# A two-layer trunk with a mixture of experts: last products ahead of three row norms ordered by row block

## The chip, the cores and the metric

The kernel runs on one core of a Trainium2 chip, and the metric is the time of one execution in microseconds (us), median over the runs. All weights come from HBM in each execution.

## The reference

256 rows of 1024 channels pass two layers. Only the parts around the three norms that the change touches are written out:

```python
x = x + mla_attention(rms_norm(x, attn_norm[0]), ...)      # ends in o @ w_o
h = rms_norm(x, ffn_norm[0])                                # n1
x = x + (silu(h @ w1) * (h @ w3)) @ w2                      # dense, 2816 wide
h = rms_norm(x, attn_norm[1]); hkv = rms_norm(x, kv_norm)   # n2, one root for both
q, k, v = h @ w_q, hkv @ w_k, hkv @ w_v                     # each 1024 x 1024
x = x + attention(q, k, v) @ w_o
h = rms_norm(x, ffn_norm[1])                                # n3
x = x + top2_of_8_experts(h)                                # each 3584 wide
# rms_norm(x, g) = x / sqrt(mean(x*x) + 1e-6) * g, over the row
```

## The kernel before

**Numbers.** Products are made of split floats. A value is its high half (what fits the fast format `fp32r`) plus a low half; `mm3` (L1370) makes each product of three: high by high, high by low, low by high. Weights come in units of 128 x 2048 (1 MB), numbered in order of use: `U_WO0` (9) begins the first output projection, `U_FFN` (13) the dense FFN, `U_L1` (46) the q, k and v projections, `U_MOE - 4` (58) the second output projection, `U_MOE` (62) the experts. SyncE loads unit n into one of six buffers `raw`, when `lo(n - 6)` is done. `hi(n)` on ScalarE (L596) writes the unit's high half into one of three slots (six from U_MOE on), when the products that used the slot are done (`unit_used`); `lo(n)` on VectorE (L919) writes the low half; `ready(n)` lets TensorE wait for `lo(n)`.

**Rows.** The 256 rows are two blocks t of 128. The residual stream is `xr`. A norm (`norm(m)` on GpSimd, n1 to n3 for m = 1 to 3) runs so: `add_residual` on VectorE adds four PSUM banks, in the order (columns 0 to 511, t=0), (same, t=1), (512 on, t=0), (512 on, t=1); ScalarE squares each block's whole row with a sum into `ss` (L605); GpSimd makes the root of it in two steps (L488, L489); VectorE multiplies the block into `tn` (`normalise`, L925); TensorE transposes 2 x 8 squares into four PSUM banks (`turn`, L1365), the banks being handed on when both blocks are in; `turn_out` takes them out with the gain, high halves on ScalarE (L616) into `hth`, low halves on VectorE (L938) into `htl`. The queues of all engines are in order and written out by hand; there is no scheduler.

**Products before the norms.** `out_proj` runs over its four units (two column halves n, two depth halves h), both blocks in each; bank 4 + 2n + t holds the sums. The dense FFN runs eleven steps: `up(c)` uses two units, `down(c)` one; at step c TensorE does `up(c + 1)` and then `down(c)`, so that `f_gate`, `f_hi` and `f_lo` of c + 1 lie beside `down(c)`. The low half `f_lo` (L1136) stands behind a `lo` on VectorE. After n2, TensorE does the q projection (units U_L1 to U_L1 + 3), then k and v from `h2h`, `h2l`: a second set of halves with the gain of `kv_norm`, taken out of the same banks (L784, L1157), ahead of `hi` and `lo` of unit U_L1 + 2. After n3 come 16 router products (L1645), the choice of experts in small VectorE steps, the gathering of an expert's rows by products (L1667, `gathered`, L834 and L1204), and the runs of the experts. In a run, `combine` (L1693) puts the preceding expert's rows back in four parts over two banks; parts three and four wait for VectorE's adds of `add_run` (L1304), which stand behind the four `lo`s of units U_MOE + 4 to + 7.

Of the kernel before, what the change touches and what calls it, by code (L numbers as in the profile page):

```python
# [20 lines left out]
P = 128  # L21
D = 1024
SEQ = 256
T = SEQ // P
# [76 lines left out]
def trunk_kernel(nc, x, attn_norm, ffn_norm, w_dq, g_cq, w_uq, w_dkv, g_ckv, w_ukv, g_qn, g_kn, w_oa,  # L101
# [25 lines left out]
    with ctx:  # L127
# [212 lines left out]
        TURN = {"n0": 0, "a0": 1, "n1": 2, "n2": 3, "a1": 4, "n3": 5}  # L340
# [132 lines left out]
        def _(pool):  # L473
# [105 lines left out]
        def _(act):  # L579
# [27 lines left out]
            def turn_out(name, dsts):  # L607

                k = TURN[name]
                for b in range(TURN_BANKS):  # L610
                    act.wait_ge(tr_done, TURN_BANKS * k + b + 1)
                    for cc in range(2):
                        c = 2 * b + cc
                        for dst, g in dsts:
                            kw = {} if g is None else {"scale": gcol[:, g + c:g + c + 1]}
                            last = nc.scalar.activation(dst[:, c, :], ps[b][:, cc * SEQ:(cc + 1) * SEQ], ACT.Copy, **kw)  # L616
                    last.then_inc(th_done, 1)

            sum_squares(0, True)
# [4 lines left out]
            turn_out("n0", [(hth, G_ATT)])  # L624
# [142 lines left out]
            with act.Fori(0, (FSTEPS - 1) // 2) as j:  # L767
                for u in range(2):
# [5 lines left out]
                    f_hi(j * 2 + (u + 1), 1 - u)  # L774
            hi(U_L1 + 1)

            sum_squares(2, False)
            turn_out("n2", [(hth, G_ATT + DC)])

            for c in range(DC):  # L780
                if c % 2 == 0:

                    act.wait_ge(tl_done, TURN_BANKS * TURN["n2"] + c // 2 + 1)
# [28 lines left out]
            turn_out("a1", [(hth, None)])  # L812
# [90 lines left out]
        def _(dve):  # L903
# [18 lines left out]
            def normalise(m):  # L922
                for t in range(T):
                    dve.wait_ge(rstd_done, T * m + t + 1)
                    nc.vector.tensor_scalar(tn[:, t, :], xr[:, t, :], rstd[:, t:t + 1], None, ALU.mult).then_inc(tn_done, 1)  # L925

            def turn_out(name, dsts):
                k = TURN[name]
                for b in range(TURN_BANKS):
                    dve.wait_ge(th_done, TURN_BANKS * k + b + 1)  # L930
                    for cc in range(2):
                        c = 2 * b + cc
                        src = ps[b][:, cc * SEQ:(cc + 1) * SEQ]
                        for h, l, g in dsts:
                            if g is None:
                                last = nc.vector.tensor_tensor(l[:, c, :], src, h[:, c, :].bitcast(fp32), ALU.subtract)
                            else:
# [885 lines left out]
```

## Time and profile before

| | |
|---|---|
| median of 3 runs | 1520.61 us (1520.49 to 1523.8) |
| the profiled execution's own time | 1523.13 us |
| its span, first to last instruction | 1521.3 us |
| mean granted clock of TensorE | 0.977 |
| TensorE busy | 1451.0 us (95%) |
| VectorE busy | 1148.2 us (75%) |
| ScalarE busy | 954.7 us (63%) |
| GpSimd busy | 42.7 us (3%) |
| DMA | 424.67 MB, 279 GB/s mean; weight units land 5.1 to 7.3 us after issue |

"PE" is TensorE, "PEld" its weight loads, "DVE" VectorE, "ACT" ScalarE, "POOL" GpSimd, "SP" SyncE. A clock of 1.00 is 2.4 GHz, 0.50 is 1.2 GHz. Times on a timeline count from the start of the span. The first third of the span holds everything up to the first expert (to about 512 us); the rest is eight expert runs of some 125 us each.

### The profile page before, as it was taken

What the parts mean: (1) busy time and instruction counts of PE and PEld (TensorE: products, weight loads), DVE (VectorE), ACT (ScalarE), POOL (GpSimd) and SP (SyncE); (2) the same over time, 40 slices, a digit from 0 to 9 for tenths busy, and PEclk for the clock granted to TensorE, in tenths of its full rate; (3) what the DMA queues carried; (4) which work ended last, traced back from release to release, by engine and by line L of the source; (5) the groups of instructions that cost most, each with busy time, mean ns of one, the idle gap of its engine ahead of it and who ended that gap; (6) DMA issues with size and microseconds to landing.
All of it is one profiled execution on the core that took longest, in us unless ns stands there. A gap on an engine that the chain in (4) does not pass through costs nothing.

```text
span 1521.3 us, 20025 instructions
## 1 busy us (share of the span) xinstructions
PE 1451.0 (95%) x7249; PEld 1217.4 (80%) x7249; DVE 1148.2 (75%) x1049; ACT 954.7 (63%) x918; POOL 42.7 (3%) x79
## 2 busy tenths in 40 slices
PE   5788999998987899999999999999999999999998
PEld 5577999997876688878878878888887887887886
DVE  4665544546674889879888888888987998888894
ACT  4455433444563677767777777687776767677772
POOL 3120000000100000000000000000000000000000
PEclk9889999998999899999999999999999999999999
DMA  8145455554532599989989999998998998999992
GB/s 303 57 122 167 138 181 181 192 188 140 185 123 86 195 337 376 372 305 375 383 320 353 375 332 331 390 360 306 379 378 326 342 382 328 339 384 332 336 376 89
DMA packets 150625, 424.67 MB, mean 279 GB/s; under 512 B 11149, under 2 KB 41018, under 8 KB 150586
## 3 DMA queue, kind: packets, MB, share of 16 engines
q1 hardware_dynamic: 146752, 420.39, 76.0%
q10 hardware_dynamic: 3450, 3.69, 0.8%
q0 software_dynamic: 384, 0.07, 0.1%
q8 instruction: 24, 0.39, 0.1%
q14 instruction: 15, 0.12, 0.0%
HBM read 423.08 MB, written 4.19 MB: 281 GB/s over the span
## 4 chain that ended last, share of the span: by engine, by line
PE 93%; DVE 4%; ACT 1%; issue 1%; POOL 0%; DMA 0%; ACTq 0%; POOLq 0%; SPq 0%; DVEq 0%
PE ps L1370 82%; PE ps L1365 4%; PE ps L1693 2%; PE ps L1667 2%; PE ps L1484 2%; PE ps L1504 1%; DVE wl_a L919 1%; ACT wh_a L596 0%; DMA xr<-in_x 0%; ACT tn L605 0%; DVE kT L1047 0%; DVE bias L1062 0%; DVE xr L955 0%; PE ps L1645 0%; DVE htl L938 0%
## 5 line engine op out<-in xcount | busy, mean ns | idle before, releaser
L919 DVE TENSOR_TENSOR wl_a<-raw,wh_a 128x2048 fp32r<-128x2048 f32 (+1 forms) x230 | 516.0, 2270 | 123.1 <-ACT wh_a L596 123.1
L596 ACT ACTIVATE wh_a<-raw 128x2048 fp32r<-128x2048 f32 (+1 forms) x230 | 434.1, 1906 | 209.6 <-PE ps L1370 200.3
L919 DVE TENSOR_TENSOR wl_b<-raw,wh_b 128x2048 fp32r<-128x2048 f32 x168 | 378.8, 2286 | 35.4 <-ACT wh_b L596 34.3
L596 ACT ACTIVATE wh_b<-raw 128x2048 fp32r<-128x2048 f32 x168 | 319.3, 1925 | 56.5 <-PE ps L1370 53.3
L1370 PE MATMUL ps<-wh_a,hth 128*128 128x512 f32 (+2 forms) x576 | 226.3, 393 | 5.6 <-DVE htl L938 3.5
L1370 PE MATMUL ps<-wl_a,hth 128*128 128x512 f32 (+2 forms) x576 | 223.4, 388 | 0.0
L1370 PE MATMUL ps<-wh_a,htl 128*128 128x512 f32 (+2 forms) x576 | 223.4, 388 | 0.0
L1370 PE MATMUL ps<-wh_b,hth 128*128 128x512 f32 x448 | 178.4, 398 | 0.0
L1370 PE MATMUL ps<-wh_b,htl 128*128 128x512 f32 x448 | 174.6, 390 | 0.0
L1370 PE MATMUL ps<-wl_b,hth 128*128 128x512 f32 x448 | 174.4, 389 | 0.0
L1370 PEld LDWEIGHTS ps<-wh_a,hth 128*128 128x128 f32 x576 | 109.3, 190 | 30.1 <-issue 6.7
L1370 PEld LDWEIGHTS ps<-wh_a,htl 128*128 128x128 f32 x576 | 109.2, 190 | 21.6
L1370 PEld LDWEIGHTS ps<-wl_a,hth 128*128 128x128 f32 x576 | 109.4, 190 | 20.5
L854 ACT ACTIVATE gth<-ps 128x512 fp32r<-128x512 f32 x56 | 30.8, 595 | 139.5 <-PE ps L1365 139.5
L1370 PE MATMUL ps<-hth,wh_a 128*128 128x256 f32 x352 | 100.5, 286 | 1.1 <-DVE htl L938 1.1
L1370 PE MATMUL ps<-htl,wh_a 128*128 128x256 f32 x352 | 100.4, 285 | 0.0
L1370 PE MATMUL ps<-hth,wl_a 128*128 128x256 f32 x352 | 100.3, 285 | 0.0
L1370 PEld LDWEIGHTS ps<-wl_b,hth 128*128 128x128 f32 x448 | 84.2, 188 | 18.9 <-issue 1.9
L1370 PEld LDWEIGHTS ps<-wh_b,hth 128*128 128x128 f32 x448 | 84.1, 188 | 18.9 <-issue 1.9
L1370 PEld LDWEIGHTS ps<-wh_b,htl 128*128 128x128 f32 x448 | 84.1, 188 | 17.6
L1370 PE MATMUL ps<-wh_b,gth 128*128 128x512 f32 x224 | 88.0, 393 | 1.3 <-DVE gtl L1285 1.3
L1370 PE MATMUL ps<-wh_b,gtl 128*128 128x512 f32 x224 | 87.3, 390 | 0.0
(230 smaller groups left out, 2050.9 us busy)
## 6 DMA issues: line engine op xcount, KB each, us to landing
raw<-in_moe_w SPq DMA_DIRECT2D x336, 1024.0 KB, 7.3
raw<-in_ffn_w SPq DMA_DIRECT2D x33, 1024.0 KB, 5.3
raw<-in_a_w_o SPq DMA_DIRECT2D x4, 1024.0 KB, 5.7
raw<-in_b_w_q SPq DMA_DIRECT2D x4, 1024.0 KB, 5.1
raw<-in_kv_w_k SPq DMA_DIRECT2D x4, 1024.0 KB, 5.1
raw<-in_kv_w_v SPq DMA_DIRECT2D x4, 1024.0 KB, 5.0
raw<-in_b_w_o SPq DMA_DIRECT2D x4, 1024.0 KB, 5.2
bias<-bias_wide ACTq DMA_DIRECT2D x8, 384.0 KB, 3.2
```

Source lines behind the costliest of these rows:

```text
L596: nc.scalar.activation(dst[:, 0:w], raw[:, n % RAW, 0:w], ACT.Copy).then_inc(hi_done, 1)
L854: last = nc.scalar.activation(gth[:, b * 512:(b + 1) * 512], ps[6 + b][:, :], ACT.Copy)
L919: nc.vector.tensor_tensor(l[:, 0:w], raw[:, n % RAW, 0:w], h[:, 0:w].bitcast(fp32), ALU.subtract).then_inc(lo_done, 1)
L1365: return nc.tensor.transpose(dst, src, ident[0:np_, 0:np_])
L1370: last = mm(dst, b if flip else a, a if flip else b, start=start and i == 0, stop=stop and i == 2)
L1484: last = mm(ps[2 + h][:, lo_:lo_ + keys], qT[part, par, q_at + t * P:q_at + (t + 1) * P], kT[part, par, h * SEQ:h * SEQ + keys], start=Tru ...
L1504: last = mm(dst, probT[:, par, h, (t + kt) * P:(t + kt + 1) * P], v_src[:, kt:kt + 1, ds(p * 2 + h, 1), v_at:v_at + VDIM], start=kt == 0, ...
L1667: last = mm(ps[7 - g][:, cc * P:(cc + 1) * P], tn[:, t, c * P:(c + 1) * P], pick[:, t, :], start=t == 0, stop=t == T - 1)
L1693: mm(ps[6 + i % 2][:, :], cmb[:, t * P:(t + 1) * P], ye[:, n * 512:(n + 1) * 512], start=True, stop=True).then_inc(m_cmb, 1)
```

## The change

- `turn_part` turns one block; a `turn_out` can be for one block; `TURN` counts n1 to n3 as two turns each. The banks are those of before.
- Squares are taken by half rows, each after its add; GpSimd scales the first half's sum ahead and adds the second's.
- In `out_proj`, unit 0 serves both blocks, units 1 to 3 block 0, then 1 to 3 block 1; block 0's transposes stand ahead of the last of these.
- In the FFN, `up` of the last step comes ahead of both last `down`s, and these run by block; block 0's transposes stand ahead of the last quarter of them.
- The first two projection units are used by block 0 first, then come block 1's transposes, then block 1.
- Adds, norms, turn outs and some `hi` and `lo` change places; `lo(U_MOE + 1)` to `+ 3` each move back by one place in VectorE's queue.

```diff
--- before.py
+++ after.py
...
-        TURN = {"n0": 0, "a0": 1, "n1": 2, "n2": 3, "a1": 4, "n3": 5}
+        TURN = {"n0": 0, "a0": 1, "n1": 2, "n2": 4, "a1": 6, "n3": 7}
...
+            for t in range(T):
+                pool.wait_ge(ss_done, t + 1)
+                root(rstd[:, t:t + 1], ss[:, t:t + 1], D).then_inc(rstd_done, 1)
+
             def norm(m):
+
                 for t in range(T):
-                    pool.wait_ge(ss_done, T * m + t + 1)
-                    root(rstd[:, t:t + 1], ss[:, t:t + 1], D).then_inc(rstd_done, 1)
-
-            norm(0)
+                    done = T + 4 * (m - 1) + 2 * t
+                    part, whole = rstd[:, T + t:T + t + 1], rstd[:, t:t + 1]
+                    pool.wait_ge(ss_done, done + 1)
+                    chain(nc.gpsimd.tensor_scalar(part, ss[:, t:t + 1], 1.0 / D, EPS, ALU.mult, ALU.add))
+                    pool.wait_ge(ss_done, done + 2)
+                    chain(nc.gpsimd.tensor_scalar(whole, ss[:, T + t:T + t + 1], 1.0 / D, part, ALU.mult, ALU.add))
+                    nc.gpsimd.tensor_tensor(whole, whole, negh[:, 0:1], ALU.pow).then_inc(rstd_done, 1)
...
-            def sum_squares(m, first):
-                for t in range(T):
-                    if first:
-                        act.wait_ge(x_here, 16 * T)
-                    else:
-
-                        act.wait_ge(xr_done, 4 * (m - 1) + 3 + t)
-                    nc.scalar.activation(tn[:, t, :], xr[:, t, :], ACT.Square, accum_out=ss[:, t:t + 1]).then_inc(ss_done, 1)
-
+            def half_squares(m, t, n):
+
+                act.wait_ge(xr_done, 4 * (m - 1) + 2 * t + n + 1)
+                piece = slice(n * 512, (n + 1) * 512)
+                nc.scalar.activation(tn[:, t, piece], xr[:, t, piece], ACT.Square,
+                                     accum_out=ss[:, n * T + t:n * T + t + 1]).then_inc(ss_done, 1)
+
+            def turn_out(name, dst, g, t=None):
...
-            turn_out("a0", [(hth, None)])
-            for n in range(U_WO0 + 2, U_FFN + 2):
-                hi(n)
-
-            sum_squares(1, False)
+            turn_out("a0", hth, None)
+            hi(U_WO0 + 2)
+            hi(U_WO0 + 3)
+            half_squares(1, 0, 0)
+            half_squares(1, 0, 1)
+            hi(U_FFN)
+            half_squares(1, 1, 0)
+            turn_out("n1", hth, G_FFN, 0)
+            hi(U_FFN + 1)
+            half_squares(1, 1, 1)
             hi(U_FFN + 2)
-            turn_out("n1", [(hth, G_FFN)])
+            turn_out("n1", hth, G_FFN, 1)
...
+            half_squares(2, 0, 0)
+            half_squares(2, 0, 1)
             hi(U_L1 + 1)
-
-            sum_squares(2, False)
-            turn_out("n2", [(hth, G_ATT + DC)])
+            turn_out("n2", hth, G_ATT + DC, 0)
+            half_squares(2, 1, 0)
+            half_squares(2, 1, 1)
+            turn_out("n2", hth, G_ATT + DC, 1)
...
+            half_squares(3, 0, 0)
+            half_squares(3, 0, 1)
+            half_squares(3, 1, 0)
+
+            act.wait_ge(unit_used, U_MOE - 1)
+            hi(U_MOE, w=UNIT)
+            turn_out("n3", hth, G_FFN + DC, 0)
+            half_squares(3, 1, 1)
+            turn_out("n3", hth, G_FFN + DC, 1)
             act.wait_ge(unit_used, U_MOE)
-            hi(U_MOE, w=UNIT)
-            sum_squares(3, False)
-            hi(U_MOE + 1, w=UNIT)
-            turn_out("n3", [(hth, G_FFN + DC)])
-            for k in range(2, 4):
+            for k in range(1, 4):
                 hi(U_MOE + k, w=UNIT)
...
+            def add_piece(t, n, done, value):
+
+                dve.wait_ge(done, value)
+                piece = xr[:, t, n * 512:(n + 1) * 512]
+                nc.vector.tensor_tensor(piece, ps[4 + 2 * n + t][:, :], piece, ALU.add).then_inc(xr_done, 1)
...
-            for n in range(U_WO0 + 1, U_FFN + 2):
+            turn_out("a0", hth, htl, None)
+            for n in range(U_WO0 + 1, U_FFN):
                 lo(n)
-            add_residual(0, U_WO0 + 4, U_WO0 + 2)
-            normalise(1)
+            add_piece(0, 0, y_done[0], 1)
+            add_piece(0, 1, y_done[0], 2)
+            normalise(1, 0)
+            add_piece(1, 0, unit_used, U_WO0 + 2)
+            lo(U_FFN)
+            turn_out("n1", hth, htl, G_FFN, 0)
+            add_piece(1, 1, unit_used, U_WO0 + 4)
+            lo(U_FFN + 1)
+            normalise(1, 1)
+            turn_out("n1", hth, htl, G_FFN, 1)
             lo(U_FFN + 2)
-            turn_out("n1", [(hth, htl, G_FFN)])
...
+            add_piece(0, 0, y_done[1], 1)
+            add_piece(0, 1, y_done[1], 2)
+            normalise(2, 0)
+            add_piece(1, 0, y_done[1], 3)
+            turn_out("n2", hth, htl, G_ATT + DC, 0)
+            add_piece(1, 1, unit_used, U_L1)
             lo(U_L1 + 1)
-            add_residual(1, U_L1)
-
-            normalise(2)
-            turn_out("n2", [(hth, htl, G_ATT + DC)])
+            normalise(2, 1)
+            turn_out("n2", hth, htl, G_ATT + DC, 1)
...
-            add_residual(2, U_MOE, U_MOE - 2)
+            add_piece(0, 0, y_done[2], 1)
+            add_piece(0, 1, y_done[2], 2)
+            normalise(3, 0)
+            add_piece(1, 0, unit_used, U_MOE - 2)
+            turn_out("n3", hth, htl, G_FFN + DC, 0)
+            add_piece(1, 1, unit_used, U_MOE)
             lo(U_MOE, w=UNIT)
-            normalise(3)
-            lo(U_MOE + 1, w=UNIT)
-            turn_out("n3", [(hth, htl, G_FFN + DC)])
+            normalise(3, 1)
+            turn_out("n3", hth, htl, G_FFN + DC, 1)
...
-            lo(U_MOE + 2, w=UNIT)
+            lo(U_MOE + 1, w=UNIT)
...
-            lo(U_MOE + 3, w=UNIT)
             gathered(0)
+            lo(U_MOE + 2, w=UNIT)
...
+            lo(U_MOE + 3, w=UNIT)
...
+            def turn_part(name, t, sem_, value, part):
+
+                pe.wait_ge(sem_, value)
+                for b in range(TURN_BANKS):
+                    for cc in range(2):
+                        c = 2 * b + cc
+                        last = tr(ps[b][:, cc * SEQ + t * P:cc * SEQ + (t + 1) * P], tn[:, t, c * P:(c + 1) * P])
+                    if part:
+                        last.then_inc(tr_done, 1)
...
+                ready(u0)
+                for t in range(T):
+                    last = piece(0, t)
+                last.then_inc(unit_used, 1)
+
+                for i in range(1, 4):
+                    ready(u0 + i)
+                    last = piece(i, 0)
+                    if i != 2:
+                        last.then_inc(y_done[2 * la], 1)
+                for i in range(1, 4):
+                    if i == 3:
+                        turn_part(then, 0, tn_done, 4 * la + 3, True)
+                    piece(i, 1).then_inc(unit_used, 1)
...
+            turn_part("n1", 1, tn_done, 4, True)
...
-            with pe.Fori(1, (FSTEPS - 1) // 2) as j:
+            with pe.Fori(1, (FSTEPS - 1) // 2 - 1) as j:
                 for u in range(2):
                     ffn_step(j * 2 + u, u, U_FFN + 2 + 3 * u, j=j, j_units=6)
-            down(FSTEPS - 1, 0, U_L1 - 1, False, True)
-
-
-            turn("n2", [(tn_done, 5), (tn_done, 6)])
-            i = 0
+            ffn_step(FSTEPS - 3, 0, U_FFN + 2 + 3 * (FSTEPS - 3))
+            up(FSTEPS - 1, 0, U_FFN + 2 + 3 * (FSTEPS - 2))
+
+
+            for t in range(T):
+                for c, par, n in ((FSTEPS - 2, 1, U_L1 - 2), (FSTEPS - 1, 0, U_L1 - 1)):
+                    if t == 0:
+                        ready(n)
+                        pe.wait_ge(f_gl, c + 1)
+                    wh, wl = split_slot(n)
+                    for half in range(2):
+                        for f in range(2):
+                            g = slice(f * SEQ + t * P, f * SEQ + (t + 1) * P)
+                            at = f * D + half * 512
+                            last = mm3(ps[4 + 2 * half + t][:, :], fgh[:, par, g], fgl[:, par, g],
+                                       wh[:, at:at + 512], wl[:, at:at + 512], False, c == FSTEPS - 1 and f == 1)
+                        if c == FSTEPS - 1 and (half, t) != (1, T - 1):
+                            last.then_inc(y_done[1], 1)
+                        if c == FSTEPS - 1 and t == T - 1 and half == 0:
+
+                            turn_part("n2", 0, tn_done, 5, True)
+                    if t == T - 1:
+                        last.then_inc(unit_used, 1)
+            def project(w, n, h, t):
...
+            for h in range(2):
+                ready(U_L1 + h)
+                project(0, 0, h, 0)
+            turn_part("n2", 1, tn_done, 6, True)
+            for h in range(2):
+                project(0, 0, h, 1).then_inc(unit_used, 1)
...
+            out_proj(1, U_MOE - 4, "n3")
+
+
+            turn_part("n3", 1, tn_done, 8, True)
...
```

## Rows read from the trace of the kernel before

**Rows 1.** Page, chain that ended last, shares of the span by engine

```profile
PE 93%; DVE 4%; ACT 1%; issue 1%; POOL 0%; DMA 0%; ACTq 0%; POOLq 0%; SPq 0%; DVEq 0%
```

**Rows 2.** The chain in order of time: start us, us, what

```profile
352.96 62.52 PE ps L1370 x264
...
611.68 16.34 PE ps L1370 x72
```

**Rows 3.** Timeline of TensorE at n1: start, us, instruction, count, [idle before, released by]

```profile
151.79 1.09 PE L1365 MATMUL ps<-cst,tn 128*128 128x128 f32 x8 [3.72 <-DVE tn L925]
153.27 1.97 PE L1365 MATMUL ps<-cst,tn 128*128 128x128 f32 x8 [0.38 <-DVE tn L925]
156.35 0.55 PE L1370 MATMUL ps<-hth,wh_a 128*128 128x256 f32 x1 [1.11 <-DVE htl L938]
```

**Rows 4.** Timeline of TensorE at n2

```profile
348.64 3.68 PE L1365 MATMUL ps<-cst,tn 128*128 128x128 f32 x16 [3.63 <-DVE tn L925]
352.96 0.77 PE L1370 MATMUL ps<-wh_a,hth 128*128 128x512 f32 x1 [0.65 <-DVE htl L938]
```

**Rows 5.** Timeline of TensorE at n3

```profile
488.96 3.68 PE L1365 MATMUL ps<-cst,tn 128*128 128x128 f32 x16 [5.80 <-DVE tn L925]
493.51 0.37 PE L1645 MATMUL ps<-hth,wrs 128*16 128x256 f32 x1 [0.87 <-DVE htl L938]
```

**Rows 6.** Stretches: length, busy by engine, granted clock, DMA share, GB/s

```profile
346.00:348.00 2.00, 0.00 (x0) 0.00 (x0) 0.47 (x2) 1.92 (x4) 0.74 (x2) 0.96 1.04 407
358.00:360.00 2.00, 2.00 (x9) 1.63 (x9) 1.46 (x2) 0.81 (x1) 0.00 (x0) 0.98 0.03 8
```

**Rows 7.** Timeline of ScalarE, n2 and after: a square, a copy

```profile
345.74 1.06 ACT L605 ACTIVATE tn<-xr 128x1024 f32<-128x1024 f32 x1 [4.15 <-DVE xr L955]
...
366.55 0.60 ACT L797 ACTIVATE q_all<-ps 128x512 f32<-128x512 f32 x1 [3.46 <-PE ps L1370]
```

**Rows 8.** Timeline of GpSimd, n2 and n3

```profile
346.97 0.19 POOL L488 TENSOR_SCALAR rstd<-ss 128x1 f32<-128x1 f32 x1 [194.54 <-ACT tn L605]
347.25 0.55 POOL L489 TENSOR_TENSOR rstd<-rstd,negh 128x1 f32<-128x1 f32 x1
...
486.24 1.25 POOL L488 TENSOR_SCALAR rstd<-ss 128x1 f32<-128x1 f32 x1 [44.13 <-ACT tn L605]
```

**Rows 9.** Timeline of VectorE, n2 and n3: adds, normalise, a `lo`

```profile
343.82 2.48 DVE L955 TENSOR_TENSOR xr<-ps,xr 128x512 f32<-128x512 f32 x4
347.83 0.75 DVE L925 TENSOR_SCALAR tn<-xr,rstd 128x1024 f32<-128x1024 f32 x1 [1.53 <-POOL rstd L489]
...
485.15 2.29 DVE L919 TENSOR_TENSOR wl_a<-raw,wh_a 128x2048 fp32r<-128x2048 f32 x1 [1.25 <-ACT wh_a L596]
```

**Rows 10.** Timelines of VectorE and ScalarE, last FFN steps: `lo(U_L1)`, `f_lo(10)`, `hi(U_L1+1)`

```profile
336.09 2.30 DVE L919 TENSOR_TENSOR wl_a<-raw,wh_a 128x2048 fp32r<-128x2048 f32 x1 [1.17 <-ACT wh_a L596]
338.30 0.69 DVE L1136 TENSOR_TENSOR fgl<-fg,fgh 128x512 fp32r<-128x512 f32 x1
...
339.67 1.92 ACT L596 ACTIVATE wh_a<-raw 128x2048 fp32r<-128x2048 f32 x1 [3.09 <-PE ps L1370]
```

**Rows 11.** Timeline of ScalarE after n2: the second set of high halves

```profile
353.94 3.07 ACT L784 ACTIVATE h2h<-ps,gcol 128x256 fp32r<-128x256 f32 x8
```

**Rows 12.** Timeline of ScalarE, first expert: high halves of gathered rows

```profile
508.06 1.14 ACT L834 ACTIVATE hth<-ps,gcol 128x128 fp32r<-128x128 f32 x4 [6.87 <-PE ps L1667]
```

**Rows 13.** Timeline of VectorE, first expert: `lo(U_MOE+3)`, gathered rows, two `lo`s, `add_run`

```profile
506.81 2.29 DVE L919 TENSOR_TENSOR wl_b<-raw,wh_b 128x2048 fp32r<-128x2048 f32 x1
...
511.20 1.13 DVE L1204 SCALAR_TENSOR_TENSOR htl<-ps,gcol,hth 128x128 fp32r<-128x128 f32 x4 [0.84 <-ACT hth L834]
...
515.64 4.64 DVE L919 TENSOR_TENSOR wl_b<-raw,wh_b 128x2048 fp32r<-128x2048 f32 x2 [1.78 <-ACT wh_b L596]
...
524.61 1.50 DVE L1304 TENSOR_TENSOR xr<-ps,xr 128x512 f32<-128x512 f32 x2
```

**Rows 14.** Timeline of TensorE, first expert: `combine`

```profile
523.50 3.83 PE L1693 MATMUL ps<-ye,cmb 128*128 128x512 f32 x8
```

More of the change, by code:

```diff
@@ L920, in lo, with normalise @@
                                         ALU.subtract).then_inc(lo_done, 1)
[L922 to L928, printed above, removed]
+            def normalise(m, t):
+                dve.wait_ge(rstd_done, T * m + t + 1)
+                nc.vector.tensor_scalar(tn[:, t, :], xr[:, t, :], rstd[:, t:t + 1], None, ALU.mult).then_inc(tn_done, 1)
@@ L940, in turn_out @@
-                    last.then_inc(tl_done, 1)
-            def add_residual(block, used, first_half=None):
-                for n in range(2):
-                    for t in range(T):
-                        i = 2 * n + t
-                        if i == 3:
-                            dve.wait_ge(unit_used, used)
-                        elif n == 0 and first_half is not None:
-                            dve.wait_ge(unit_used, first_half)
-                        else:
-                            dve.wait_ge(y_done[block], i + 1 if first_half is None else 1)
-                        piece = xr[:, t, n * 512:(n + 1) * 512]
-                        nc.vector.tensor_tensor(piece, ps[4 + i][:, :], piece, ALU.add).then_inc(xr_done, 1)
@@ L957, in _ @@
-            normalise(0)
+                        part = slice(lo_, lo_ + n_)
+                        src = ps[b][:, cc * SEQ + lo_:cc * SEQ + lo_ + n_]
+                        if g is None:
+                            last = nc.vector.tensor_tensor(l[:, c, part], src, h[:, c, part].bitcast(fp32), ALU.subtract)
+                        else:
+                            last = nc.vector.scalar_tensor_tensor(l[:, c, part], src, gcol[:, g + c:g + c + 1],
+                                                                  h[:, c, part].bitcast(fp32), ALU.mult, ALU.subtract)
@@ L1371, in mm3, with turned @@
                 return last
[L1373 to L1384 removed]
+            def turn_part(name, t, sem_, value, part):
[6 more added lines that the diff above has]
+                        last.then_inc(tr_done, 1)
+            def turned(name, c=DC - 1, first=True, t=0):
                 if first:
[L1387 removed]
+                    pe.wait_ge(tl_done, TURN_BANKS * (TURN[name] + t) + c // 2 + 1)
             def ready(n, j=0, j_units=0):
@@ L1394, in _ @@
             pe.wait_ge(c_here, 16)
-            turn("n0", [(tn_done, 1), (tn_done, 2)])
+            for t in range(T):
+                turn_part("n0", t, tn_done, t + 1, t == T - 1)
             pe.wait_ge(g_here, 16 * 5)
@@ L1558, in _ @@
             for _ in attention(0):
                 pass
-            turn("a0", 2 * [(A[0]["oo"], PAIRS)])
-            out_proj(0, U_WO0)
-            turn("n1", [(tn_done, 3), (tn_done, 4)])
+            for t in range(T):
+                turn_part("a0", t, A[0]["oo"], PAIRS, t == T - 1)
+            out_proj(0, U_WO0, "n1")
+            turn_part("n1", 1, tn_done, 4, True)
             def up(c, par, n, j=0, j_units=0, first=False):
@@ L1590, in down @@
                                        wh[:, at:at + 512], wl[:, at:at + 512], first and f == 0, last_ and f == 1)
-                        if last_ and (half, t) != (1, T - 1):
-                            last.then_inc(y_done[1], 1)
                 last.then_inc(unit_used, 1)
@@ new lines, in _ @@
+            for t in range(T):
+                for c, par, n in ((FSTEPS - 2, 1, U_L1 - 2), (FSTEPS - 1, 0, U_L1 - 1)):
[15 more added lines that the diff above has]
+                        last.then_inc(unit_used, 1)
@@ new lines, in project @@
+            def project(w, n, h, t):
+                xh, xl = (hth, htl) if w == 0 else (h2h, h2l)
+                i = 4 * w + 2 * n + t
+                wh, wl = split_slot(U_L1 + 4 * w + 2 * n + h)
+                if h == 0:
+                    free_bank(i, 1)
+                for cc in range(4):
+                    c = 4 * h + cc
+                    turned("n2", c, w == 0 and n == 0 and c % 2 == 0, t)
+                    if w == 1 and n == 0 and t == 0 and c % 2 == 0:
+                        pe.wait_ge(h2_done, c // 2 + 1)
+                    last = mm3(ps[4 + i % 4][:, :], xh[:, c, t * P:(t + 1) * P], xl[:, c, t * P:(t + 1) * P],
+                               wh[:, cc * 512:(cc + 1) * 512], wl[:, cc * 512:(cc + 1) * 512], c == 0, c == DC - 1)
+                return last
```

96 lines of the change are left out of this document (33 added, 63 removed).

## The prediction

> **What bounds the kernel now.** I read the page's chain of work by engine first [rows 1]: TensorE holds 93% of it, so only stretches in which TensorE waits, or runs at the lower clock, can give time back. The chain in order of time gives the price of a product at full clock: 72 of 512 columns in 16.34 us, 0.227 us each [rows 2]. Twelve of them, half a weight unit for one row block, I call a piece: 2.72 us. Then the timeline of TensorE at the three seams where a row norm follows the last products; the idle time in front of the transposes tells when those products ended:
> - FFN norm (n1): end at 151.79 - 3.72 = 148.07, first `up` product at 156.35 [rows 3]: 8.28 us.
> - second layer's attention norm (n2): end 345.01, first projection product 352.96 [rows 4]: 7.95 us.
> - MoE norm (n3): end 483.16, first router product 493.51 [rows 5]: 10.35 us.
>
> Together 26.6 us, of which only the 16 transposes of each are work. The stretches at n2 show the clock too: it falls from 2.4 towards 1.2 GHz while TensorE is idle (mean 0.96 over 346 to 348) and is back at 358 (0.98) [rows 6]. The projections from 352.96 took 62.52 us for 264 products without a break, where 264 x 0.227 = 59.9 [rows 2]: 2.6 us of slow clock. The 16 transposes took 3.68 us there [rows 4], against 1.09 for eight at full speed [rows 3], 1.5 more.
>
> **Prices.** A square over 1024 columns holds ScalarE 1.06 us; a half lies between half of that, 0.53, and the 0.60 of a 128x512 copy [rows 7]; I take 0.6, and 0.1 for the sum. GpSimd's two steps are 0.19 and 0.55 [rows 8]. Normalise is 0.75 per block; four adds are 2.48 [rows 9], one alone I put at 0.7. The high halves of a 128x128 turn out took 1.14 for four [rows 12]; a block has eight, 2.3 us on ScalarE, and VectorE follows one pair behind. A `hi` is 1.92 [rows 10], a `lo` 2.29 [rows 9], 2.25 in a series.
>
> GpSimd's 0.19 us step took 1.25 us at 486.24, to 487.49 [rows 8], and the `lo` that VectorE had begun at 485.15 ended at 487.44 [rows 9]: beside a `lo` this step waits for its end. The change puts a `lo` between the last add and the last scaling of all three seams, and I count that wait; were the row an accident, the sum would be 2.1 us lower (a rival below). The Trainium skill has it as a rule, in SBUF — State Buffer, Who interferes with whom: a VectorE instruction with two SBUF inputs keeps out a GpSimd one that reads SBUF. By that rule, the trace agrees.
>
> **n1.** The new order keeps the eight pieces and makes block 0's last one the fifth, which ends at 148.07 - 3 x 2.72 = 139.9. Its add, half square, root and normalise end near 143.1, ahead of the seventh piece's end at 145.35; so the block's eight transposes (1.0 to 1.1 us) stand between products, and the last product ends at E = 149.1. After E: add to E+0.75, `lo(U_FFN+1)` to E+2.95 (its `hi` runs on ScalarE from 147.9 to 149.8), and though the square is there at E+1.5, GpSimd is kept out till E+2.95; root to E+3.55, normalise to E+4.3. Then block 1's transposes, a first bank of 0.5 at the slow clock, ScalarE's pair 0.6, VectorE's pair 0.6, with hand-overs 1.95 to 2.0: first `up` product at E+6.3 = 155.4. Gain 0.95. The other order bound: no transposes hidden and no shorter chain, nothing.
>
> **n2.** `up(10)` ends at 345.01 - 10.9 (two `down`s of 5.44) = 334.1. Then come both last `down`s for block 0, and both for block 1. The second for block 0 needs `f_lo(10)`, which stands behind `lo(U_L1)` on VectorE and ends at 338.99 [rows 10]; before, the whole of `down(9)`, 5.4 us, was its cover, now half of it, to 336.8: a new stall of 2.3 us. From 339.1, block 0's two column halves end at 340.4 and 341.8 and its norm is ready at 345.2; `down` of block 1 runs on to 345.8, the transposes to 346.8, the last half of it to 348.2, 3.2 later than before. ScalarE turns block 0 out from 346.5 (behind `hi(U_L1+1)`), so the first projection piece runs 348.2 to 350.9. The second needs `lo(U_L1+1)`, now behind block 0's turn out and the last add on VectorE: 350.0 to 352.25. TensorE waits 1.45 and runs to 355.1. Block 1 is normalised at 353.6, kept out as above; its transposes end at 356.1, TensorE waits 0.7 for its turn out, and its two pieces run 356.8 to 362.2. What is late next: `h2h`, `hi` and `lo` of unit U_L1+2, which stand behind block 1's turn out. ScalarE: turn out 355.5 to 357.8, `h2h` 3.0 [rows 11], `hi` 1.9, to 362.7; `lo` to 365.0. That unit's products start at 365.1, where they started at 352.96 + 2 x 5.44 + 2.6 = 366.5. Gain 1.4, of the 4.3 us by which the pieces before it were early.
>
> **n3.** As n1, but `hi(U_MOE)` (1.9) runs ahead of block 0's turn out on ScalarE, which ends at 484.7, VectorE's at 485.3. Last product 484.2, one set of transposes later; add 485.3 to 486.0, `lo(U_MOE)` to 488.2, GpSimd kept out till then, root 488.8, normalise 489.55, first router product 489.6 + 1.95 = 491.5. Gain 2.0.
>
> **First expert.** Here I expect n3's gain to be given back. The `lo`s of units U_MOE+1 to +3 each move back by one place. Before, `lo(U_MOE+3)` ran at 506.81 [rows 13], while VectorE had to wait for ScalarE's part of the gathered rows (508.06 [rows 12]) anyway; nothing takes its place. Now two `lo`s, 4.5 us, stand between `gathered(0)` and the run, where VectorE was idle for 1.78 [rows 13]. On the old clock: gathered rows done 512.3, `lo` 514.6, gates 1.55, `lo` 518.4, four `lo`s of 2.25 to 527.4. Behind them is `add_run`, which began at 524.61 [rows 13]. In TensorE's `combine`, eight products in 3.83 us from 523.50 [rows 14], the third pair waits for the first add and the fourth for the second. So it ends near 528.2 + 1.95 = 530.1 instead of 527.33: 2.8 us lost. The register loads ahead of the run's loop lay in the 1.78 us of idleness and no longer do: 0 to 1.8 us, 0.3 taken, as an engine's hand-overs in these rows are nearer to nothing. Loads of units U_MOE+8 on start up to 9 us later, but lie several units ahead of their use; nothing, and if that cover were gone a load's landing (5 to 7 us on the page). The two more squares of each norm and GpSimd's extra 0.19 us step lie in pauses of their engines and cost nothing; on the path each would be 0.6 and 0.2.
>
> **Sum.** -0.95 - 1.4 - 2.0 + 2.8 + 0.3 = -1.3 us. The profiled execution took 1523.13 us, its span 1521.3; the sum against its own time is 1521.8. The median of the runs is 1520.61, 2.5 below it; where that lies I can't show (the runs spread over 3.3 us, about what a slow clock at one seam costs). Forecast by the median: 1519.3.
>
> **Rivals.**
> - *The first expert's backlog doesn't reach TensorE*: 3.1 less, 1516.2. For: VectorE had 1.78 us of idleness there. Against: from 506.8 on I count 17.3 us of work for it where 15.1 stood. 18%.
> - *GpSimd isn't kept out by a `lo`*: n1 ends 0.75 earlier, n3 1.35, n2 the same: 1517.2. Against: the 1.25 us row [rows 8]. 7%.
> - *Slower: the clock falls in the new stall of n2.* The price is that of n2's slow stretch now, 2.6 us [rows 2], or 4.1 with the transposes; 3.4 taken: 1522.7. It decides whether the clock falls at all at a stall of 2.3 us between dense products. For: it fell after a pause of 3.72 us with only transposes behind it (the second eight took 1.97 [rows 3]). Against: that pause was longer. 15%. The Trainium skill (TensorE: Matmul & The Clock Gate, Why this matters for your kernels) warns of pauses longer than this one; by it the clock would hold, and no row here shows a pause of this length.
> - *The change doesn't do what it says*: block 0 is early, but block 1's chain is as long as the old one and no seam gains: 1520.6 + 3.1 = 1523.7. Against: that chain has half a square and half a turn in it. 10%.
>
> The forecast has 50%. A measurement of this kernel can tell about 0.3%, 4.6 us, from no change: the bounds are 1516.05 and 1525.2. Faster: half of the first rival and some of the second and of the forecast's low end, 0.13. Slower: the high ends of the last two (4.1, and register loads of 1.8), 0.06. Within it, 0.81. The range of 1515.8 to 1523.8 reaches to the first rival and to the last.
>
> **What would show it.** Right: TensorE idle for 2.3 us ahead of block 0's second `down`, behind `fgl`; 1.5 us behind `wl_a` between the two first projection pieces, and near 3 us ahead of unit U_L1+2; GpSimd's last scaling in n1 and n3 ending with a `lo`; the first expert's `combine` waiting near 3 us for `xr`. Wrong: a `combine` without that wait, a granted clock below 1 from 339 on, or block 0's transposes waiting for their normalise.

## The result: slower than forecast, and slower than before

| | before | after |
|---|---|---|
| timed together with the first profile | 1521.83 us | 1526.95 us (1526.3 to 1527.64, 6 runs) |
| ratio | | 1.0034, 95% interval [1.0022, 1.0045] |
| timed again, beside the kernel before | 1522.18 us | 1525.64 us (1524.51 to 1526.94, 11 runs), 1.0021 [1.0012, 1.003] |
| profiled execution, span | 1523.13, 1521.3 | 1526.84, 1525.0 |
| mean granted clock | 0.977 | 0.982 |

The forecast was 1519.3, with a range to 1523.8: wrong in sign, and the time lies outside. The slowdown is small, 0.2 to 0.3%, but both intervals lie above 1. Yet nearly every wait that the forecast listed is in the trace. At n1, TensorE's timeline of the changed kernel (start, us, instruction, [idle before, released by]) and below it GpSimd's last scaling and VectorE's `lo`:

```profile
146.51 1.03 PE L1394 MATMUL ps<-cst,tn 128*128 128x128 f32 x8
154.85 1.97 PE L1394 MATMUL ps<-cst,tn 128*128 128x128 f32 x8 [4.57 <-DVE tn L945]
156.99 0.55 PE L1399 MATMUL ps<-hth,wh_a 128*128 128x256 f32 x1 [0.17 <-DVE htl L959]
...
151.94 1.43 POOL L503 TENSOR_SCALAR rstd<-ss,rstd 128x1 f32<-128x1 f32 x1 [3.60 <-ACT tn L610]
...
150.94 2.29 DVE L939 TENSOR_TENSOR wl_a<-raw,wh_a 128x2048 fp32r<-128x2048 f32 x1
```

They answer to [rows 3]: block 0's transposes stand between products with no wait. From the last product (154.85 - 4.57 = 150.28) to the first `up` product are 6.71 us, where 6.3 were forecast and 8.28 stood before. GpSimd's step ends at 153.37, 0.14 behind the `lo`. At n3, which answers to [rows 5], it is 7.60 us for 10.35:

```profile
491.42 1.97 PE L1394 MATMUL ps<-cst,tn 128*128 128x128 f32 x8 [5.46 <-DVE tn L945]
493.56 0.37 PE L1717 MATMUL ps<-hth,wrs 128*16 128x256 f32 x1 [0.17 <-DVE htl L959]
```

At n2, which answers to [rows 4], TensorE waits four times, for 6.4 us together:

```profile
339.13 0.47 PE L1399 MATMUL ps<-wh_a,fgh 128*128 128x512 f32 x1 [2.28 <-DVE fgl L1156]
354.02 0.50 PE L1399 MATMUL ps<-wh_a,hth 128*128 128x512 f32 x1 [1.23 <-DVE wl_a L939]
358.64 0.50 PE L1399 MATMUL ps<-wh_a,hth 128*128 128x512 f32 x1 [0.71 <-DVE htl L959]
366.60 0.50 PE L1399 MATMUL ps<-wh_a,hth 128*128 128x512 f32 x1 [2.22 <-DVE wl_a L939]
```

In the first expert, `add_run` begins only as the fourth `lo` of the run ends, at 526.7, and `combine` waits for it; these rows of VectorE and TensorE answer to [rows 13, 14]:

```profile
522.30 4.48 DVE L939 TENSOR_TENSOR wl_a<-raw,wh_a 128x2048 fp32r<-128x2048 f32 x2
526.71 1.28 DVE L1333 TENSOR_TENSOR xr<-ps,xr 128x512 f32<-128x512 f32 x2
...
527.44 3.30 PE L1765 MATMUL ps<-ye,cmb 128*128 128x512 f32 x4 [2.47 <-DVE xr L1333]
```

What the forecast doesn't have is in the granted clock. The stretches of the changed kernel (length, busy by engine, then granted clock, DMA share, GB/s) behind the first, the fourth and the combine's wait:

```profile
340.00:341.00 1.00, 1.00 (x5) 0.77 (x4) 0.00 (x0) 0.00 (x0) 0.00 (x0) 0.62 0.76 256
341.00:343.00 2.00, 2.00 (x6) 1.52 (x5) 0.69 (x1) 0.72 (x2) 0.19 (x1) 0.50 0.96 375
344.00:346.00 2.00, 2.00 (x10) 1.67 (x9) 0.37 (x1) 0.72 (x2) 0.62 (x2) 1.00 0.00 0
...
366.00:367.00 1.00, 0.40 (x2) 0.36 (x3) 1.00 (x2) 1.00 (x3) 0.00 (x0) 1.00 0.00 0
368.00:370.00 2.00, 2.00 (x6) 1.51 (x6) 2.00 (x3) 0.31 (x1) 0.00 (x0) 0.50 0.76 295
372.00:374.00 2.00, 2.00 (x10) 1.66 (x9) 0.00 (x0) 0.00 (x0) 0.00 (x0) 1.00 1.05 386
...
526.00:527.00 1.00, 0.00 (x0) 0.00 (x0) 1.00 (x2) 1.00 (x2) 0.00 (x0) 1.00 0.94 365
528.00:531.00 3.00, 3.00 (x6) 1.33 (x5) 0.91 (x2) 0.00 (x0) 0.00 (x0) 0.50 1.02 407
532.00:534.00 2.00, 2.00 (x11) 1.62 (x10) 2.00 (x2) 0.10 (x1) 0.00 (x0) 1.00 0.67 274
```

Three times TensorE goes on at full clock for 0.5 to 1.1 us after the wait, is granted 0.50 (1.2 GHz) while its work is dense, and comes back after some 3.4 us. Over 341 to 343 the row counts 6 products where it otherwise counts 10 or 11.

Do such falls come in dense work anyway? Two long stretches of the changed kernel, of the dense FFN and of the experts, answer that; in them TensorE is busy all the time:

```profile
162.50:335.00 172.50, 172.50 (x1242) 163.70 (x1241) 82.19 (x51) 68.85 (x52) 0.00 (x0) 1.00 0.56 184
535.00:1494.00 959.00, 959.00 (x4400) 787.39 (x4400) 827.49 (x573) 694.72 (x521) 0.00 (x0) 1.00 0.95 352
```

The granted clock is 1.00 in both, and so it is in the same stretches of all 18 profiles of this case.

**The span in sections.** To sum this, I cut each profile at six products of TensorE and its end: the first of the first output projection, the first `up` product (n1), the first of the second output projection (n2), the first of the router (n3), the first of the first expert, and the first behind its `combine`. Mean over four profiles of the kernel before and five of the changed order (one with its last loop steps written out, see below), in us; the spread of each in brackets (a page gives the span to 0.1 us, so the last section is good to 0.05):

| section | before | after | difference | forecast |
|---|---|---|---|---|
| to the output projection | 126.40 (126.07-126.87) | 126.78 (125.78-127.73) | +0.4 | 0 |
| n1 | 30.29 (30.28-30.31) | 29.63 (29.62-29.65) | -0.66 | -0.95 |
| dense FFN, n2, attention | 304.59 (302.93-305.82) | 306.06 (305.24-307.02) | +1.47 | -1.4 |
| n3 | 32.38 (32.37-32.39) | 30.53 (30.51-30.53) | -1.85 | -2.0 |
| router, gathering | 18.89 (18.68-19.01) | 18.62 (18.16-19.38) | -0.27 | 0 |
| first expert up to its `combine` | 14.29 (14.29-14.30) | 17.54 (16.80-17.91) | +3.25 | +3.1, with the next |
| the rest | 994.58 (994.54-994.64) | 995.14 (994.57-995.39) | +0.56 | |

The sum is +2.9, for +3.5 and +5.1 timed. The first section is code that the change doesn't touch, and its two spreads overlap.

### The profile page after: what moved, and what is told of

It is laid out like the page before. It is cut to its first block, busy times and chain, and to the rows that moved or that the text cites. A ratio compares the mean times of both kernels' runs of the same rounds, so it can differ in the third digit from the quotient of the medians.

```text
span 1525.0 us, 20089 instructions
## 1 busy us (share of the span) xinstructions
PE 1450.9 (95%) x7249; PEld 1214.9 (80%) x7249; DVE 1151.2 (75%) x1073; ACT 960.3 (63%) x954; POOL 47.7 (3%) x85
## 4 chain that ended last, share of the span: by engine, by line
PE 91%; DVE 5%; ACT 2%; issue 1%; DMA 1%; POOL 0%; DVEq 0%; ACTq 0%; POOLq 0%; SPq 0%
PE ps L1399 80%; PE ps L1394 4%; PE ps L1765 2%; PE ps L1739 2%; PE ps L1513 2%; DVE wl_a L939 1%; PE ps L1533 1%; ACT wh_a L604 1%; DVE htl L959 1%; DMA xr<-in_x 0%; ACT hth L621 0%; DVE kT L1060 0%; DVE bias L1075 0%; PE ps L1717 0%; DMA bias<-bias_wide 0%
```

## The experiments

All but five were timed in 5 to 11 runs of their own beside 16 to 27 of the kernel before, whose median was 1522.13 to 1522.34; a profiled execution of each gives the sections. "Below" is below the changed kernel's 1525.64. The other five are one profiled execution each.

**The kernel before, again** (one profiled execution).

> The kernel before, once more, for a second profile. In the first one the chain reached the first output projection at 126.07 us, in the changed kernel's profile at 127.34, with nothing of the change ahead of it. If that 1.3 us is chance (where the slow clock falls in the unchanged start), this profile will show another start, anywhere from 125.5 to 128.5, while the stretch from that first output product to the first up product stays at 30.3 us and the one from there to the router's first product at 337.2, each within the 2 us that a slow clock can take. If it belongs to the change, the start stays within 0.3 us of 126.07.

1524.74 us, span 1522.9. The start is 126.57 for 126.07, more than the 0.3 that would have tied it to the change, so it varies by itself. The section with n2 is 305.82 for 304.79; the granted clock fell at places where nothing had changed (424.5 and 458.5 us).

**`f_lo(10)` ahead of `lo(U_L1)`.** The last two FFN steps of ScalarE's and VectorE's loop are written out and two instructions change places in the last one (excerpt, against the written-out form):

```diff
-                lo(n + 2, FSTEPS // 2 - 1, 6)
                 f_lo(FSTEPS - 2 + u, 1 - u)
+                lo(n + 2, FSTEPS // 2 - 1, 6)
```

(for u = 1, where n + 2 is U_L1; `hi` and `f_hi` alike).

> The changed kernel, with the high and low halves of the last FFN step's gated product taken ahead of the hi and lo of unit U_L1 instead of behind them (the last two steps of two loops written out for it). Theory 1, the clock falls after the 2.3 us stall ahead of block 0's second down: stall and slow stretch both go, the granted clock stays 1.00 from 330 to 350, block 0's second down ends 3.9 us earlier (2.3 of stall, 1.6 of slow clock), and the kernel takes 1526.95 - 3.9 = 1523.0 us, unless the wait ahead of unit U_L1+2 grows by as much. Theory 2, the slow stretch there was chance and would come anyway: 2.3 us less, 1524.7. If neither the stall nor the clock was on the path (the chain of block 1's turn out sets it): 1526.95.

1519.7 us (1518.95 to 1521.1), ratio 0.9984 [0.9975, 0.9993]: 5.9 below, far more than the wait of 2.3 that is gone. TensorE's timeline has no wait behind `fgl`, and in this execution the clock held behind the other two as well, though they are still there. The wait at unit U_L1 + 2, and then the stretch behind it:

```profile
362.03 0.50 PE L1419 MATMUL ps<-wh_a,hth 128*128 128x512 f32 x1 [2.21 <-DVE wl_a L949]
```

```profile
363.00:365.00 2.00, 2.00 (x10) 1.64 (x10) 2.00 (x3) 0.73 (x1) 0.00 (x0) 1.00 0.71 257
```

The section with n2 is 302.16 us. My expectation counted the wait and one fall; in the profile two more falls are missing. From the first output projection product on, this profile is 4.3 below the mean of the changed order's five; 1.6 of the 5.9 isn't in it.

**`lo(U_MOE + 2)` back ahead of the gathered rows.**

```diff
-            gathered(0)
             lo(U_MOE + 2, w=UNIT)
+            gathered(0)
```

> The changed kernel, with lo(U_MOE+2) back in VectorE's idle time ahead of the gathered rows, where lo(U_MOE+3) stood before the change. Theory 1 (the backlog of two lo behind the gathered rows reaches combine): add_run begins 2.2 us earlier, the wait of 2.47 us inside the first combine falls to some 0.3, and since the clock no longer falls behind that wait another 1 to 1.5 us comes back: 1526.95 - 3.6 = 1523.3. Theory 2 (only the wait, the slow clock comes anyway): 1524.8. If combine is set by something else: 1526.9, and the wait stays.

1521.73 us, 0.9993 [0.9984, 1.0002]: 3.9 below. VectorE's `lo` fills the time in which it waited for ScalarE, and the combine's wait is 0.27 (timelines of VectorE and TensorE):

```profile
505.29 2.29 DVE L939 TENSOR_TENSOR wl_a<-raw,wh_a 128x2048 fp32r<-128x2048 f32 x1
507.51 1.13 DVE L1232 SCALAR_TENSOR_TENSOR htl<-ps,gcol,hth 128x128 fp32r<-128x128 f32 x4
...
523.75 1.98 PE L1765 MATMUL ps<-ye,cmb 128*128 128x512 f32 x4 [0.27 <-DVE xr L1333]
```

The last two sections together are 1009.23, and in before 1008.83 to 1008.93. So all but 0.4 us of the backlog is that one `lo`.

**n2 in the old order** (both last `down`s, all transposes, then the projection; squares by half rows and everything at n1 and n3 kept).

> The changed kernel with the second seam (end of the FFN, norm n2, first two projection units) ordered as before, n1 and n3 as changed. In the changed kernel's profile n2 is worth +1.4 us against before, by two stalls of 2.2 to 2.3 us and two slow stretches that cost 1.6 us each. Theory 1: so this one takes 1526.95 - 1.4 = 1525.5, a little more or less by the chance of one slow stretch in the old order. Rival (n2 gained its 1.4 us as predicted, and the loss is elsewhere): 1528.4.

1523.13 us, 1.0007 [0.9998, 1.0016]: 2.5 below, where my theory had 1.4 and its rival a loss. Its n2 section, 302.64, is under before's too. With the squares by half rows the chain is shorter: the wait ahead of the transposes is 2.78 for 3.63 [rows 4], and the first eight of these ran at full clock (timeline of TensorE):

```profile
346.21 1.10 PE L1392 MATMUL ps<-cst,tn 128*128 128x128 f32 x8 [2.78 <-DVE tn L944]
348.04 1.86 PE L1392 MATMUL ps<-cst,tn 128*128 128x128 f32 x8 [0.73 <-DVE tn L944]
350.56 0.77 PE L1397 MATMUL ps<-wh_a,hth 128*128 128x512 f32 x1 [0.65 <-DVE htl L958]
```

By the split into clock and remainder that is made below, the clock is what this section gained: 4.0 us lost to it for 6.6 in before, and a remainder of 298.6 for 297.8 to 298.3.

**The changed kernel again, and a control** with the same loop steps written out and the order left as it is.

> The changed kernel once more, beside the kernel before on the same chip. If the 5 us by which it came out slower belong to its code, the ratio is again 1.003 (some 1526.5 us for 1522). If a part of them belongs to the start of that one chip (its first output projection stood 1.3 us later than in the kernel before, in code that the change does not touch), the ratio is 1.001 to 1.002. In its profile the stall at the first gate product of the last unit is 2.3 us, the one at unit U_L1+2 2.2 and the combine's 2.5; where the granted clock falls to 0.5 behind one of them it stays there for 3.4 us.

> The changed kernel with the loops of its last steps written out and the order of every instruction left as it is: the control for the kernels whose steps were reordered. It computes and issues the same, so every theory expects the time of the changed kernel within 0.1%. If it is 2 us faster, then the 1519.7 of the kernel with f_lo first was partly the written-out form.

1525.64 us and 1526.21 us (1.0024 [1.0015, 1.0033]): writing the steps out gives nothing. The two have the same order, and yet the clock held behind `fgl` in the changed kernel's profile and fell in the control's (from each, the wait and the stretch behind it):

```profile
339.01 0.47 PE L1399 MATMUL ps<-wh_a,fgh 128*128 128x512 f32 x1 [2.28 <-DVE fgl L1156]
340.00:343.00 3.00, 3.00 (x15) 2.47 (x14) 1.38 (x2) 0.97 (x3) 0.19 (x1) 1.00 0.88 333
...
339.60 0.47 PE L1413 MATMUL ps<-wh_a,fgh 128*128 128x512 f32 x1 [2.35 <-DVE fgl L1163]
341.00:344.00 3.00, 3.00 (x9) 2.35 (x8) 0.69 (x1) 0.72 (x2) 0.19 (x1) 0.50 0.77 298
```

**GpSimd left free.** `lo(U_FFN + 1)` at n1 and `lo(U_MOE)` at n3 stand behind block 1's splits (excerpt, the one at n1):

```diff
-            lo(U_FFN + 1)
             normalise(1, 1)
             turn_out("n1", hth, htl, G_FFN, 1)
+            lo(U_FFN + 1)
```

> The changed kernel with lo(U_FFN+1) of the first norm and lo(U_MOE) of the third moved behind block 1's splits, so that VectorE runs no cast-and-subtract while GpSimd has its last scaling. If that scaling is 1.43 and 1.40 us long because VectorE's split keeps GpSimd out, it falls to 0.2 to 0.3 us, the last normalise starts about 1.2 us earlier, and block 1's turns in both norms too: 0.8 to 1.2 us at each, 1.6 to 2.4 less than the changed kernel in all, if nothing else is late. The rival (GpSimd's step is long of itself) leaves the time as it is.

1523.31 us, 1.0002 [0.9993, 1.0011]: 2.3 below. GpSimd's scaling falls from 1.43 to 0.27, and the wait ahead of block 1's transposes from 4.57 to 3.41 (timelines of GpSimd and TensorE):

```profile
152.22 0.27 POOL L503 TENSOR_SCALAR rstd<-ss,rstd 128x1 f32<-128x1 f32 x1 [3.60 <-ACT tn L610]
...
153.97 1.97 PE L1394 MATMUL ps<-cst,tn 128*128 128x128 f32 x8 [3.41 <-DVE tn L945]
```

n3 gains the same (29.40 us for 30.53). By the Trainium skill (SBUF — State Buffer, Who interferes with whom) a VectorE instruction with two SBUF inputs contends with a GpSimd one that reads SBUF. By that rule, the trace agrees: only the two `lo`s moved, and the scaling fell by 1.16 us.

**Unit U_L1 + 2 split ahead of block 1's turn out**, loops written out as in the control (excerpt).

```diff
+            lo(U_L1 + 2)
             turn_out("n2", hth, htl, G_ATT + DC, 1)
```

(`hi` alike, and both left out of the loop behind).

> The changed kernel with one thing moved: hi and lo(U_L1+2), the split of the third projection unit, stand ahead of block 1's turns instead of behind block 1's splits. In the changed kernel the unit's first product waits 2.2 us for it, and the clock fell to 0.5 for 3.4 us behind that wait in each of its profiles. If that is 2.2 + 1.7, the time is 3.5 to 4 below the changed kernel's, 1521.5 to 1522, and the section from the first up product to the second attention's output projection 302 instead of 305.2 to 306.0. The rival (the split moved ahead makes block 1's turns or splits late by as much): no change.

1522.63 us, 1.0003 [0.9994, 1.0012]: 3.0 below, and the n2 section is 301.28 for 305.24 in the changed kernel's second profile, in neither of which the clock fell at the first wait. The 4.0 are the wait of 2.2 and one fall, 1.7; why the runs gave 1 less than this pair of profiles stays open.

**Two orders together** (`f_lo` first, `lo(U_MOE + 2)` back).

> f_lo first and lo(U_MOE+2) back ahead of the gathered rows, nothing else. Alone they came out 5.9 and 3.9 us below the changed kernel (1519.7 and 1521.7 for 1525.6). If their stalls and the clock behind them add up: 1515.8 and, against the fastest, 3 us are left for unit U_L1+2 and GpSimd's steps. The rival (the gains overlap, since f_lo first also kept the clock up at the combine by moving it in time): 1517.3, the combine's 2.5 alone being added.

1517.33 us (1516.49 to 1518.07), 0.9969 [0.9957, 0.9981]: 8.3 below, where 9.8 would be the sum, and just what the rival expected: a part of what `f_lo` first gained was the clock at the combine. The one profile of `f_lo` first agrees; its other ten runs can't show it. Here the clock fell behind the 2.19 us at unit U_L1 + 2, as it had not with `f_lo` first alone (the wait and the stretch behind it):

```profile
360.92 0.50 PE L1419 MATMUL ps<-wh_a,hth 128*128 128x512 f32 x1 [2.19 <-DVE wl_a L949]
362.00:365.00 3.00, 3.00 (x9) 2.33 (x8) 3.00 (x3) 0.62 (x1) 0.00 (x0) 0.50 0.94 318
```

**All four.**

> All reorderings together: f_lo(10) first, lo(U_MOE+2) back ahead of the gathered rows, hi and lo(U_L1+2) ahead of block 1's turns, and the two splits that keep GpSimd out moved behind. My theory (the change gains 0.6 and 1.9 us at the first and third norm and loses it all to three stalls that it opens itself, of 2.2 to 2.5 us each, and to the clock that falls behind them): without the three stalls 1518.5 us, with the two splits moved another 1 to 2, 1517 to 1518, 0.3% faster than before. The rival (the loss is spread, or a stall comes back elsewhere): 1520 to 1522.

1512.82 us (1512.18 to 1514.13), 0.9934 [0.992, 0.9948]: faster than both kernels, by more than I expected (1517 to 1518). The four taken alone add up to 15.1 below; together they are 12.8. Its timeline at n2 has two waits left, and the clock stays up (the stretch behind the first):

```profile
349.09 0.50 PE L1423 MATMUL ps<-wh_a,hth 128*128 128x512 f32 x1 [1.14 <-DVE wl_a L951]
353.70 0.50 PE L1423 MATMUL ps<-wh_a,hth 128*128 128x512 f32 x1 [0.70 <-DVE htl L971]
```

```profile
350.00:352.00 2.00, 2.00 (x11) 1.58 (x10) 2.00 (x2) 0.00 (x0) 0.00 (x0) 1.00 0.95 225
```

Its sections: n1 28.26, n2 300.15, n3 29.38, expert 14.61, rest 994.58.

**The same without one of the four.**

> All reorderings at the first norm, the third and the experts as in the fastest kernel so far (1512.8), but the second norm in its old order (all last products, then all turns, then the projection; squares by half rows kept). That section was 302.6 us long in the kernel with this order alone and 300.15 in the fastest, so the block order of the second norm, with its stalls mended, is worth 2.5: 1515.3. The rival (without its stalls the block order is worth nothing, and the difference was the other edits): 1512.8 to 1513.5.

> The fastest kernel with lo(U_MOE+2) put back behind the gathered rows, so that the first combine waits for xr again. The wait itself is 2.5 us; in the changed kernel's four profiles the clock fell behind it, and it cost 4.1 to 4.3 from the first expert product on; in the two kernels where it did not fall, 2.5. So 1515.3 without a fall, 1517 with one, and the section from the first expert product to the first linear product 16.8 or 17.7 us for 14.6.

n2 in the old order: 1516.6 us (1514.69 to 1517.59), 3.8 slower than the fastest (2.5 expected), so the block order there is good once its long waits are gone. The profiles show less of it: 301.48 us for the section, beside 300.15 with all four and 298.24 in the kernel below, which has the same order at n2. `lo(U_MOE + 2)` behind the gathered rows: 1516.69 us (1514.88 to 1519.72), 3.9 slower; the combine waits 2.46 and the clock falls, sections 17.74 and 995.22 (the wait and the stretch behind it):

```profile
517.32 3.35 PE L1789 MATMUL ps<-ye,cmb 128*128 128x512 f32 x4 [2.46 <-DVE xr L1357]
518.00:521.00 3.00, 3.00 (x6) 1.36 (x5) 0.99 (x2) 0.00 (x0) 0.00 (x0) 0.50 1.03 416
```

**Two more profiles of each kernel**, for what the sections left open.

> The kernel before, one more profile. Both its profiles so far came from executions above its median (1523.13 and 1524.74 for 1522.2), with 10 us at half clock behind the second norm or with falls in dense work. If such executions are the exception, the section from the first up product to the second attention's output projection is 302.6 to 304 us here instead of 304.8 and 305.8, with 7 us at half clock, and the whole from the first up product on 1394 or less instead of 1395.2 and 1396.3. If they are the rule, 304.8 or more.

> As the one above: the kernel before, to see how the clock behind the second norm varies from one execution to the next.

> The changed kernel, one more profile. Its profiles gave 305.2 to 306.0 us from the first up product to the second attention's output projection, the clock falling at unit U_L1+2 in each, and at the first stall in two of three; and 1396.7 to 1397.8 from the first up product on. The theory expects the same here, and the fall at the combine again.

> As the one above: the changed kernel, to see whether a fall behind one of its three stalls is ever missing.

1521.89, 1523.18, 1526.16 and 1525.54 us. The n2 section took 302.93 and 304.82 in before, 305.95 and 307.02 in the changed kernel; so of before's four profiles three are the longer kind and one the shorter. From the first output projection product on, before takes 1393.2 to 1396.3 us in four profiles and the changed kernel 1396.7 to 1397.9 in five: they don't overlap. The sections account for 2.9 us; 0.6 of one timed difference and 2.2 of the other stay open. In the last profile the clock held at the combine, and that shows what a fall costs there. Stretches of it, to be put beside 528 to 531 above:

```profile
526.00:528.00 2.00, 0.29 (x1) 0.29 (x2) 2.00 (x3) 2.00 (x2) 0.00 (x0) 1.00 0.94 356
529.00:531.00 2.00, 2.00 (x9) 1.39 (x8) 1.83 (x3) 0.00 (x0) 0.00 (x0) 1.00 1.02 420
```

## Why the prediction was wrong, by its own steps

The forecast's base was low: a median of three runs, 1520.61, where more runs gave 1521.8 to 1522.3. So 1.2 us or more of the miss is none of the change's. What the change itself did was forecast at -1.3 and came out at +3.5 and +5.1.

**The waits were right.** Stall behind `fgl`: 2.3 forecast, 2.28. Wait for `lo(U_L1 + 1)`: 1.45, 1.23. Block 1's turn out: 0.7, 0.71. Unit U_L1 + 2: from 362.2 to 365.1, near 3; measured 2.22. `combine`: near 3, measured 2.47. GpSimd kept out: 1.43, 1.40, 1.40 us at the three norms, and shown at n1 and n3 by the kernel that frees it, so that rival falls. So does the one of a backlog that doesn't reach TensorE, and the one by which no seam gains. n1 gave 0.3 less: block 1's transposes began 4.57 behind the last product for 4.3, and from them to the first `up` product it took 2.14 for 1.95 to 2.0. n3 gave 0.15 less.

**The step that failed is the price of a wait between dense products.** The sum took each new wait at its own length. Three of them, of 2.2 to 2.5 us, stand with full work on both sides, and the clock fell behind most: over all profiles of all kernels that have the wait, behind `fgl` in 5 of 8, at unit U_L1 + 2 in 8 of 9, at the combine in 7 of 10. One of the forecast's own signs of being wrong, a granted clock below 1 from 339 on, came true. The size is plain at the combine, where little else varies. The last two sections are 1008.83 to 1008.93 in before, 1011.37 to 1011.41 in the three profiles with the wait and no fall, 1012.93 to 1013.10 in the seven with both. The wait is 2.5, the fall 1.6: 3.4 us at half clock. The forecast had 3.1 there: 0.6 too much for the wait, and nothing for the fall, 1.6.

**n2: the gain was a gain of clock.** Adding up (1 - granted clock) x length over stretches of half a microsecond gives what each section lost at the lower clock; in the n2 section it is 5.1 to 7.5 in before's profiles (mean 6.6) and 3.9 to 6.2 in the changed kernel's (4.7). The remainder is 297.8 to 298.3 before and 300.8 to 301.5 after. (`f_lo` first, alone and with the `lo` back, has one order at n2 and gave 298.2 and 298.9, so this split is good to some 0.7.) So waits cost 3.3 more, and the clock gave 1.9 back. The sum holds the end of the fall behind n1 too, which reaches over the cut; behind n2 itself before lost 5.1 in all four profiles and the changed kernel 1.7 to 5.1, in the mean 3.4. And some 0.7 of before's 5.1 fell on time in which TensorE stood idle: by this estimate the waits cost 2.6 more and the clock gave 1.2 back. The forecast's own numbers are +2.7 for the waits (1.4 less than 4.1, which were the slow clock's part of projection and transposes) and -4.1 for the clock. The waits were right; it let the whole slow stretch go and put two waits in its place that bring most of it back. That is the larger part of the error: n2 came out at +1.5 for -1.4, the first expert and the rest at +3.8 for +3.1.

**The slower rival was the right mechanism at one place out of three.** I gave it 15% and the stall at 339 alone. Had it stood at all three waits, with the 1.6 us that a fall proved to cost for the 3.4 that I took from [rows 2] and [rows 4], it would have given -1.3 + 3 x 1.6 = +3.5. That this is one of the two timed differences is partly luck: the other is +5.1, the sections give +2.9, and the clock didn't fall at every wait. The argument against it was that the pauses which show a fall in the trace of before were longer (3.72 us); no row showed that one of 2.3 is safe. The Trainium skill (TensorE: Matmul & The Clock Gate, Why this matters for your kernels) warns only of idle gaps between bursts that are longer than these waits. By that rule the clock would have held; the runs here show otherwise, and the measurement decides: 20 falls behind 27 waits of 2.2 to 2.5 us.

**n3's gain was given back, as forecast, and twice over (3.8 us for 1.9), but by a choice that could be undone.** One `lo` moved over `gathered(0)` gives the 3.9 us back and costs nothing at n3.

## What to carry to other kernels

Reordering for a norm's chain bought 0.7 and 1.9 us at the two seams where nothing came late; each instruction that is thereby late for TensorE costs its wait, and at the 2.2 to 2.5 us seen here mostly 1.6 us more in clock. So price such a wait between dense products at its length plus 1.6, and look at every one, not only at the first. Reorder the queues behind the change too: the same change with the splits of five units moved in ScalarE's and VectorE's queues took 1512.8 us instead of 1525.6. Keep a `lo`, a VectorE instruction of 2.3 us with two inputs in SBUF, away from the moment when GpSimd has a short step on the path: 1.1 us each time.

## What the runs showed of the hardware

- The order of the code alone doesn't settle whether the clock falls behind a wait of one length: the control kernel and the changed kernel's second profile have the same order, and behind `fgl` the clock fell in the one (340.7 to 344.1) and held in the other. The kernel with `f_lo` first kept it up behind 2.21 and 2.51 us. What settles it no run here shows.
- Shorter waits in the same place were not followed by a fall: the twelve profiles with the block order at n2 have a wait of 1.1 to 1.2 us for `lo(U_L1 + 1)`, and the next fall came 12 us later or more in each.
- In 19 of the 20 cases the fall came 0.3 to 1.1 us after TensorE had resumed (in one 0.2 before); it costs 1.6 to 1.7 us with products that are otherwise dense. Two executions of before differ by 2.9 us in one section (302.93 and 305.82), 2.4 of it by what they lost at the lower clock, so a single profile can't tell a change of 1 us at such a place.
